# One third of an adaLN vector moved from TensorE's matmuls to VectorE's sums, and the attention bias rows read in two transfers, in a four-layer diffusion step

## The chip, the cores and the metric

The kernel runs on one core of a Trainium2 chip. The time is that of the whole kernel on the device, in microseconds. Each engine of the core (TensorE, VectorE, ScalarE, GpSimd, SyncE) runs its own instructions in order and waits on semaphores for the others. Transfers are issued from queues (SyncE's and GpSimd's here) and are carried by 16 DMA engines that all the queues share.

## The reference

Four layers run over 128 context tokens and 128 latent tokens of width 1024, all in float32. The part that matters here is the adaLN vector of each layer and the attention of the second layer:

```python
cond_act = jax.nn.silu(cond)                 # one vector for the context, one for the latent tokens
for i in range(DEPTH):
    mod = (cond_act @ ada_w[i] + ada_b[i])   # 1024 x 6144 weights a layer
    sh1, sc1, g1, sh2, sc2, g2 = [mod[..., n * D:(n + 1) * D] for n in range(6)]
    h = rms_norm(x, norm1_g[i]) * (1 + sc1) + sh1
    m = mixer(h)                             # pooling, attention, Fourier, pooling
    x = x + g1 * m
    h = rms_norm(x, norm2_g[i]) * (1 + sc2) + sh2
    x = x + g2 * moe(h)                      # 16 experts, top 2
```

In the attention of the second layer (16 heads of 64) the context tokens attend to each other, and a latent token attends to a window of the 2 x 64 latent grid, with a learned relative bias for each head, and to 128 cached context keys:

```python
bias = rpb[:, row_b[:, None, :, None], col_b[None, :, None, :]]
s_loc = jnp.einsum('brqhd,brkwhd->bhrqkw', q, kg) * ATTN_SCALE + bias[None]
s_loc = jnp.where(valid_col[:, None, :], s_loc, -jnp.inf)
s = jnp.concatenate([s_loc.reshape(B, N_HEADS, R, GRID_W, n_loc), s_ctx], axis=-1)
p = jax.nn.softmax(s, axis=-1)
```

## The kernel before, in words

**Weights.** All weights, 527 MB, pass once through a ring of 12 slots of 1 MB (128 partitions of 2048 columns) and seven side buffers. SyncE's queue issues the transfers in a fixed order (`BEFORE_EXPERTS` ahead of a layer's experts, `GROUP_UNITS` in them). Ahead of each transfer it waits in `room` until the slot's last unit has been used: TensorE counts units in the semaphore `s_used`, and `used(u, l, base)` says what count means that unit `u` is done. As the queue is in order, a slot that comes free late holds back all transfers behind it.

**adaLN.** The 6144 columns of a layer's vector are computed in three thirds of 2048 columns; third `t` belongs to layer `t // 3`. A third has eight ring units, one for each 128 of the 1024 input channels. `ada(t, a, b)` on TensorE multiplies units a to b - 1: four matmuls a unit, with `cact` (128 channels x 32 columns, of which the first two are the context's and the latent tokens' SiLU) as weights and 512 columns of the unit as the moving operand, accumulated in four groups of 32 rows of one bank, `B_ADA`. `ada_rows(t)` on VectorE then adds the bias (`adabr`, brought by GpSimd's queue), `ada_turn(t)` on TensorE transposes the rows and `ada_mods(t)` on VectorE writes them to `mods` (and `grow` for the gates). One bank serves all thirds, so third t + 1 waits until third t has been copied (`s_mod`).

**Attention of the second layer** (`attention` of each engine). TensorE makes queries and keys by channel (`by_channel`), values by token (`by_token`), and for each of eight pairs of heads `scores(hp)`, `turn(hp)` (transposes of the probabilities) and `attend(hp)`. VectorE adds the bias and takes the maximum (`bias_max`), ScalarE exponentiates (`exps`), VectorE normalises (`normalise`), ScalarE copies the transposed probabilities (`copy_turned`), VectorE copies the output (`copy_output`). The order on each engine is written out by hand. TensorE's order puts other matmuls between a pair's scores and its transposes: projections, and pieces of the thirds 4 to 8. After the eighth pair, `project` multiplies by the output weights in two halves of the columns (`cc`), each for the two sequences (`s`), with the gate rows (`gates`) ahead of the second sequence and half of third 8 between the column halves. Third 7 is the second third of the second layer; its result is wanted for the gate and shift that come after attention.

**Bias rows.** In the first layer the relative bias is turned around, written to memory as `bias_rows` (3 grid-row distances x 128 x 16 heads) and in the second layer read back into `braw`: partition p, the query, gets for each key row the 64 x 16 numbers that begin p % 64 rows on. Rows of neighbouring partitions overlap. GpSimd's queue does this right behind the cached keys and values (`ck`, `cv`); VectorE expands `braw` into `bias` (line 1130) ahead of the first `bias_max`.

Of the kernel before, what the change touches and what calls it, by code (L numbers as in the profile page):

```python
# [7 lines left out]
F32 = mybir.dt.float32  # L8
# [6 lines left out]
P = 128  # L15
# [38 lines left out]
def matrix_units(name, c):  # L54
# [7 lines left out]
    + matrix_units("qkv", 4) + ada_units(5) + matrix_units("qkv", 1) + ada_units(6)[:4] + matrix_units("qkv", 3) + ada_units(6)[4:]  # L62
    + matrix_units("qkv", 5) + ada_units(7) + matrix_units("wo", 0) + ada_units(8)[:4] + matrix_units("wo", 1) + ada_units(8)[4:],
# [60 lines left out]
B_ADA = B_G  # L124

# [84 lines left out]
def used(u, l, base):  # L210

    return base * NU + (u + 1 - LAYER_UNITS * l)


def build(nc, x_prompt, x_sample, cache_k, cache_v, c, c_ctx, ada_w, ada_b, norm1_g, norm2_g, pool_w,
# [4 lines left out]
    with ctx:  # L220
# [50 lines left out]
        gpair = sb("gpair", [P, GROUP, 2])  # L271

# [30 lines left out]
        with ExitStack() as at:  # L303
# [4 lines left out]
            qT = sb("qT", [P, DB, T], F32, at)  # L308
            kT = sb("kT", [P, DB, T], F32, at)
# [4 lines left out]
            sb("at_experts", [P, 64], F32, at)  # L314
# [47 lines left out]
        knew = ck  # L362

# [12 lines left out]
        s_used = sem("s_used")  # L376
        s_behind = sem("s_behind")
# [116 lines left out]
        def _(sp):  # L494
# [66 lines left out]
            def group(l, base, k):  # L561
                it = sp.snap(base + k)
                e0 = sp.snap((k & (NG - 1)) * GROUP)
                for v, (kind, e, h) in enumerate(GROUP_UNITS):
                    u = EXPERTS_AT[l] + v
                    sp.wait_ge(s_used, used(u - RING, l, it))
# [22 lines left out]
        def _(pool):  # L589
# [18 lines left out]
            nc.gpsimd.memset(rw[:, :, :], 0.0).then_inc(s_zero, 1)  # L608
            nc.gpsimd.memset(rheads[:, :, :], 0.0).then_inc(s_pad, 1)
            pool.wait_ge(s_zero, 4)  # L610
# [8 lines left out]
            pool.dma_start(bias_dram.rearrange("d p h -> p d h"), rback[:, :, :]).then_inc(s_bias, 16)  # L619
# [35 lines left out]
        def _(ac):  # L655
# [93 lines left out]
            def attention(l, base):  # L749
# [9 lines left out]

                def exps(hp):  # L760
# [16 lines left out]
                empty(Q0, blocks(qT, 0, 2))  # L777
                empty(K0, blocks(kT, 0, 2))
# [12 lines left out]
                empty(Q1A, blocks(qT, 4, 2))  # L791
# [656 lines left out]
        def _(pe):  # L1448
# [130 lines left out]
            def project(l, base, name, src, banks, between=None):  # L1579

                for cc in range(2):
                    if cc == 1 and between is not None:
                        between()
# [511 lines left out]
```

## Time and profile before

| | us |
|---|---|
| median of 3 runs | 1321.14 |
| lowest and highest run | 1320.13, 1322.42 |
| the profiled execution | 1319.5 |
| its span, first to last instruction | 1317.7 |
| TensorE busy in the span | 1247.0 (95%) |
| VectorE busy in the span | 390.7 (30%) |
| ScalarE busy in the span | 330.6 (25%) |

The profiled execution is one run of its own. Busy time counts matmuls and element-wise instructions and not waits or the issue of transfers. The memory is read at 405 GB/s over the whole span. Starts are in microseconds from the span's start.

### The profile page before, as it was taken

Reading aid. Unit: us, or ns where it says so; the run is one execution under the profiler, and the core shown is the slowest. Engines: PE = TensorE matmul, PEld = TensorE weight load, DVE = VectorE, ACT = ScalarE, POOL = GpSimd, SP = SyncE. Lnnn points to the kernel's source line nnn. Section 1 sums busy time; section 2 is a strip of 40 time slices with the busy share of each in tenths; the row PEclk is TensorE's granted clock in tenths of the full one; section 3 lists DMA queues with packets and bytes.
Section 4 is the critical chain, followed back from the end, with each engine's and each line's share of the span. In section 5 each row is a group of like instructions: output and inputs, shape, how many; then the busy total and the mean of one; then the engine's idle time right before and its main releaser. Section 6 shows DMA issues by size and latency. Waiting matters only on the chain.

```text
span 1317.7 us, 17235 instructions
## 1 busy us (share of the span) xinstructions
PE 1247.0 (95%) x6557; PEld 561.7 (43%) x6557; DVE 390.7 (30%) x882; ACT 330.6 (25%) x712; POOL 37.6 (3%) x76
## 2 busy tenths in 40 slices
PE   3979999999899999999999899999999989999996
PEld 0433434343656644443434254443434444434342
DVE  1242213222232324321332324222331452213324
ACT  1241212122221223221212233221222452212122
POOL 2100000000200000000100000000000000000000
PEclk9889999999999999999999999999999999999999
DMA  9999999999999988999999999999999999999994
GB/s 371 420 420 421 421 420 422 421 421 421 400 367 408 394 339 356 422 420 421 421 419 422 421 408 398 422 421 422 420 421 421 413 422 420 422 421 420 422 421 193
DMA packets 87278, 535.43 MB, mean 406 GB/s; under 512 B 11192, under 2 KB 13336, under 8 KB 25760
## 3 DMA queue, kind: packets, MB, share of 16 engines
q1 hardware_dynamic: 82336, 527.47, 97.4%
q0 software_dynamic: 3120, 5.17, 1.2%
q10 hardware_dynamic: 1744, 1.73, 0.4%
q8 instruction: 53, 0.87, 0.3%
q14 instruction: 25, 0.20, 0.0%
HBM read 532.20 MB, written 2.12 MB: 405 GB/s over the span
## 4 chain that ended last, share of the span: by engine, by line
PE 83%; DMA 10%; DVE 3%; ACT 2%; issue 1%; SPq 0%; DVEq 0%; ACTq 0%
PE ps L1954 31%; PE ps L2003 15%; PE ps L1940 5%; PE ps L2015 5%; PE ps L1463 5%; PE ps L1630 4%; PE ps L1592 4%; DMA ring<-in_ada_w_dram 4%; DMA ring<-in_moe_w_up_dram 3%; PE ps L1986 2%; PE ps L1639 2%; DMA ring<-in_attn_wqkv_dram 2%; DMA ring<-in_moe_w_down_dram 2%; PE ps L1560 1%; PE ps L1971 1%; ACT hT L707 1%
## 5 line engine op out<-in xcount | busy, mean ns | idle before, releaser
L1956 PE MATMUL ps<-ring,xg 128*64 128x512 f32 x968 | 438.7, 598 | 0.0
L1954 PE MATMUL ps<-ring,xg 128*64 128x512 f32 x912 | 413.2, 598 | 4.0 <-DMA ring<-in_moe_w_up_dram 4.0
L2003 PE MATMUL ps<-ring,gb 128*64 128x512 f32 x992 | 225.6, 595 | 0.3 <-DMA ring<-in_moe_w_down_dram 0.3
L1954 PEld LDWEIGHTS ps<-ring,xg 128*64 128x64 f32 x912 | 117.7, 137 | 230.0 <-issue 219.6
L1387 DVE SCALAR_TENSOR_TENSOR gb<-ps,gslot,g2x 128x512 f32<-128x512 f32 x128 | 90.2, 746 | 248.8 <-PE ps L2003 248.8
L2003 PEld LDWEIGHTS ps<-ring,gb 128*64 128x64 f32 x992 | 68.9, 137 | 134.2 <-issue 126.2
L1956 PEld LDWEIGHTS ps<-ring,xg 128*64 128x64 f32 x968 | 125.0, 137 | 0.0
L885 ACT ACTIVATE y_hi<-gb 128x512 fp32r<-128x512 f32 x128 | 77.2, 627 | 169.0 <-PE ps L2015 109.1
L1463 PE MATMUL ps<-ring,cact 128*32 128x512 f32 x768 | 94.8, 629 | 12.1 <-ACT cact L668 6.0
L872 ACT ACTIVATE gu<-ps 128x512 f32<-128x512 f32 x64 | 38.3, 598 | 247.0 <-PE ps L1956 247.0
L1396 DVE TENSOR_TENSOR y_lo<-gb,y_hi 128x512 fp32r<-128x512 f32 x128 | 83.6, 688 | 12.5 <-ACT y_hi L885 11.9
L1378 DVE TENSOR_TENSOR gb<-sg,ps 128x256 f32<-128x256 f32 x64 | 26.8, 418 | 192.7 <-ACT sg L877 192.7
L877 ACT ACTIVATE sg<-ps 128x256 f32<-128x256 f32 x64 | 24.6, 384 | 216.6 <-PE ps L1986 216.6
L2015 PE MATMUL ps<-y_hi,onehotT 64*128 64x512 f32 x256 | 57.5, 446 | 3.1 <-DVE y_lo L1396 3.1
L1404 DVE TENSOR_TENSOR gpair<-onehotT 128x8 f32<-128x8 f32 x16 | 2.7, 168 | 194.0 <-ACT onehotT L891 194.0
L1630 PE MATMUL ps<-hT,ring 128*128 128x256 f32 x256 | 58.2, 389 | 2.0 <-DMA ring<-in_attn_wqkv_dram 2.0
L1940 PE MATMUL ps<-onehot,h_hi 128*128 128x256 f32 x256 | 56.7, 304 | 3.1 <-DVE adabr L1024 3.1
L868 ACT ACTIVATE xg<-ps 128x512 f32<-128x512 f32 x64 | 38.2, 597 | 77.4 <-PE ps L1940 77.3
L1630 PEld LDWEIGHTS ps<-hT,ring 128*128 128x128 f32 x256 | 49.4, 194 | 9.7 <-issue 2.7
L1463 PEld LDWEIGHTS ps<-ring,cact 128*32 128x32 f32 x768 | 22.5, 114 | 71.4 <-issue 52.1
L1940 PE MATMUL ps<-onehot,h_lo 128*128 128x256 f32 x256 | 52.4, 287 | 0.0
L2015 PE MATMUL ps<-y_lo,onehotT 64*128 64x512 f32 x256 | 50.4, 391 | 0.0
(223 smaller groups left out, 1117.9 us busy)
## 6 DMA issues: line engine op xcount, KB each, us to landing
ring<-in_moe_w_down_dram SPq DMA_DIRECT2D x124, 1024.0 KB, 17.7
ring<-in_moe_w_up_dram SPq DMA_DIRECT2D x121, 1024.0 KB, 16.9
ring<-in_moe_w_gate_dram SPq DMA_DIRECT2D x114, 1024.0 KB, 17.9
ring<-in_ada_w_dram SPq DMA_DIRECT2D x96, 1024.0 KB, 17.9
ring<-in_attn_wqkv_dram SPq DMA_DIRECT2D x12, 1024.0 KB, 21.5
spare<-in_moe_w_down_dram SPq DMA_DIRECT2D x4, 1024.0 KB, 23.6
xh<-in_moe_w_up_dram SPq DMA_DIRECT2D x4, 1024.0 KB, 20.9
hT<-in_moe_w_gate_dram SPq DMA_DIRECT2D x4, 1024.0 KB, 22.7
```

What stands on the lines that cost most here:

```text
L872: nc.scalar.activation(gu[:, :, :], ps[:, B_GU, :].rearrange("p (m j) -> p j m", j=FB), ACT.Copy).then_inc(s_guc, 1)
L885: nc.scalar.activation(y_hi[:, s, :], y[:, s, :], ACT.Copy).then_inc(s_yh, 1)
L1387: v.scalar_tensor_tensor(y[:, s, :], ps[:, DOWN_BANKS[e % 2], :], gslot[:, e:e + 1], g2x[:, s, :], ALU.mult, ALU.mult).then_inc(s_yf, 1)
L1396: v.tensor_tensor(y_lo[:, s, :], y[:, s, :], y_hi[:, s, :].bitcast(F32), ALU.subtract).then_inc(s_y, 1)
L1463: mm = pe.matmul(ps[32 * j:32 * (j + 1), B_ADA, :], cact[:, i, :], w[:, j * 512:(j + 1) * 512], start=(i == 0 or (t, i) == (3, 4)), stop=( ...
L1592: mm = pe.matmul(ps[:, banks[2 * cc + s], :], src[4 * h + b][:, s * SEQ:(s + 1) * SEQ], w[:, b * 512:(b + 1) * 512], start=(h == 0 and b = ...
L1630: mm = pe.matmul(ps[:, JOB_BANK[i], d * T:(d + 1) * T], w[b // 4][:, at:at + P], hT[:, b, :], start=(b == 0), stop=(b == DB - 1))
L1940: mm = pe.matmul(ps[:, (B_G, B_T)[j % 2], d * 256:(d + 1) * 256], h[:, s, b * P:(b + 1) * P], onehot[:, s, :, 0:SLOTS], start=(n2 == 0), s ...
L1954: mg = pe.matmul(ps[0:SLOTS, B_GU, :], xg[:, b, e, :], wg[:, i * F:(i + 1) * F], start=(b == 0), stop=(b == DB - 1))
L1956: mu = pe.matmul(ps[SLOTS:P, B_GU, :], xg[:, b, e, :], wu[:, i * F:(i + 1) * F], start=(b == 0), stop=(b == DB - 1))
L2003: mm = pe.matmul(ps[r * SLOTS:(r + 1) * SLOTS, DOWN_BANKS[e % 2], :], acts[:, e % ACTS, j, :], w[:, i * D + r * HALF:i * D + (r + 1) * HAL ...
L2015: mm = pe.matmul(ps[:, B_ACC + 2 * s + r, :], onehotT[part, NSEQ * e + s, 0:SEQ], of[part, s, :], start=False, stop=False, skip_group_chec ...
```

## The change

Third 7 no longer runs as 32 matmuls of TensorE. VectorE multiplies each unit (128 channels x 2048 columns) by its channel's SiLU, a scalar per partition, and adds up the eight units, once for each of the two sequences, into two tiles of 128 x 2048: 2 products and 14 multiply-adds (`summed`). They are put one by one between the instructions of the softmax, from the fourth pair on. One tile is `spare`, the other the place of the first eight query and key blocks, which are no longer wanted then; queries and keys are laid out anew for that. TensorE then sums each tile over its 128 partitions with a column of ones (`reduce_sums`, 8 matmuls) inside the output projection. Slots of third 7 are freed by VectorE's count `s_summed`. The units of third 7 move forward in the ring's order, the last four units of third 6 move behind the eighth pair's scores, and the transposes of thirds 6 and 7 move with them.

The bias rows are written to memory in three transfers instead of one, in reverse order of the distance, and read in two transfers over 128 partitions (one for each key row) instead of four over 64.

```diff
 BEFORE_EXPERTS (second layer)
-    + matrix_units("qkv", 4) + ada_units(5) + matrix_units("qkv", 1) + ada_units(6)[:4] + matrix_units("qkv", 3) + ada_units(6)[4:]
-    + matrix_units("qkv", 5) + ada_units(7) + matrix_units("wo", 0) + ada_units(8)[:4] + matrix_units("wo", 1) + ada_units(8)[4:],
+    + matrix_units("qkv", 4) + ada_units(5) + matrix_units("qkv", 1) + ada_units(7)[:1] + ada_units(6)[:4] + ada_units(7)[1:3]
+    + matrix_units("qkv", 3) + ada_units(7)[3:4] + matrix_units("qkv", 5) + ada_units(7)[4:6] + ada_units(6)[4:] + ada_units(7)[6:]
+    + matrix_units("wo", 0) + ada_units(8)[:4] + matrix_units("wo", 1) + ada_units(8)[4:],
...
+        sums = [spare[:, :], first_qk[:, :, :, :].rearrange("p i b t -> p (i b t)")]
...
 SyncE, room
-                    sp.wait_ge(s_used, used(USE_OF[at - RING], l, base))
+                    u = USE_OF[at - RING]
+                    if u in SUMMED_UNITS:
+                        sp.wait_ge(s_summed, NSEQ * SUMMED_UNITS[u])
+                    else:
+                        sp.wait_ge(s_used, used(u, l, base))
...
 GpSimd
-            pool.dma_start(bias_dram.rearrange("d p h -> p d h"), rback[:, :, :]).then_inc(s_bias, 16)
+            for d in range(3):
+                pool.dma_start(bias_dram[2 - d], rback[:, d, :]).then_inc(s_bias, 16)
...
-            pool.wait_ge(s_bias, 32)
-            for r in range(2):
-                for kr in range(2):
-                    src = bass.AP(tensor=bias_dram.tensor, offset=((kr - r + 1) * P + 1) * HEADS,
-                                  ap=[[HEADS, GRID_W], [1, GRID_W * HEADS]])
-                    pool.dma_start(braw[r * GRID_W:(r + 1) * GRID_W, kr, :, :].rearrange("p k h -> p (k h)"), src).then_inc(s_bias, 16)
+            pool.wait_ge(s_bias, 64)
+            for kr in range(2):
+                src = bass.AP(tensor=bias_dram.tensor, offset=((1 - kr) * P + 1) * HEADS,
+                              ap=[[P * HEADS, 2], [HEADS, GRID_W], [1, GRID_W * HEADS]])
+                pool.dma_start(braw[:, kr, :, :].rearrange("p k h -> p (k h)"), src).then_inc(s_bias, 16)
...
 VectorE
+            def summed(i, seqs=range(NSEQ)):
+                at = place(UNIT_AT[("ada", SUMMED, i)], 1)
+                w = ring[:, at % RING, :]
+                if 0 in seqs:
+                    v.wait_ge(s_slot[at % RING], landed(at, 1, bases[1]))
+                for s in seqs:
+                    if i == 0:
+                        ins = v.tensor_scalar(sums[s], w, cact[:, i, s:s + 1], None, ALU.mult)
+                    else:
+                        v.wait_ge(s_summed, NSEQ * (i - 1) + s + 1)
+                        ins = v.scalar_tensor_tensor(sums[s], w, cact[:, i, s:s + 1], sums[s], ALU.mult, ALU.add)
+                    ins.then_inc(s_summed, 1)
...
                 normalise(3)
-                empty(Q1B, blocks(qT, 6, 2))
+                v.wait_ge(s_job, JOB_DONE[K_TURN0])
+                summed(0)
+                empty(Q1B, second(0, 2))
+                summed(1)
                 copy_output(2)
+                summed(2)
+                summed(3, [0])
                 copy_output(3)
                 bias_max(4)
+                summed(3, [1])
                 normalise(4)
-                empty(K1B, blocks(kT, 6, 2))
+                empty(K1B, second(1, 2))
+                summed(4, [0])
                 bias_max(5)
+                summed(4, [1])
                 normalise(5)
-                ada_rows(6, l, base)
+                summed(5, [0])
                 bias_max(6)
+                summed(5, [1])
                 normalise(6)
-                ada_mods(6)
+                summed(6, [0])
                 empty(V1B, vtok[:, 1, 512:1024])
+                summed(6, [1])
                 copy_output(4)
                 bias_max(7)
                 copy_output(5)
                 normalise(7)
+                ada_rows(6, l, base)
                 copy_output(6)
                 copy_output(7)
+                ada_mods(6)
+                summed(7)
                 ada_rows(7, l, base)
                 ada_mods(7)
                 projected(l, "wo", 0, (4, 5, 6, 7))
...
 TensorE
+            def reduce_sums():
+                pe.wait_ge(s_mod, SUMMED)
+                pe.wait_ge(s_summing, 2)
+                pe.wait_ge(s_summed, NSEQ * ADA_UNITS)
+                for s in range(NSEQ):
+                    for j in range(4):
+                        mm = pe.matmul(ps[32 * j:32 * (j + 1), B_ADA, :], summing[:, 31 - s:63 - s], sums[s][:, j * 512:(j + 1) * 512],
+                                       start=(s == 0), stop=(s == NSEQ - 1))
+                mm.then_inc(s_reduced, 1)
...
                 scores(5)
-                ada(6, 4, ADA_UNITS, l, base)
                 w = weights(5)
                 by_token(V1A, w, 0)
...
-                turned(K_TURN1, [kT[:, 4 + i, 0:SEQ] for i in range(4)])
-                ada_turn(6)
+                turned(K_TURN1, [kT[4 + i][:, 0:SEQ] for i in range(4)])
                 by_token(V1B, w, 1)
...
                 attend(5)
-                ada(7, 0, 6, l, base)
+                ada(6, 4, ADA_UNITS, l, base)
                 turn(7)
                 attend(6)
-                ada(7, 6, ADA_UNITS, l, base)
                 attend(7)
                 gates(l, 0)
-                ada_turn(7)
+                ada_turn(6)
                 pe.wait_ge(s_os, PAIRS)
-                project(l, base, "wo", oT, (4, 5, 6, 7), lambda: ada(8, 0, 4, l, base))
+                project(l, base, "wo", oT, (4, 5, 6, 7),
+                        {(0, 1, 0): reduce_sums, (0, 1, 1): lambda: ada_turn(7), (1, 0, 0): lambda: ada(8, 0, 4, l, base)})
```

## Rows read from the trace of the kernel before

**Rows 1.** Stretches: us, busy time of each engine, granted clock, DMA share, GB/s.

```profile
480.00:495.00 15.00, 15.00 (x45) 6.03 (x47) 1.57 (x3) 5.61 (x10) 1.63 (x4) 1.00 0.81 329
530.00:733.00 203.00, 203.00 (x1043) 83.16 (x1043) 50.73 (x105) 43.90 (x84) 3.62 (x7) 1.00 1.01 421
```

**Rows 2.** SyncE's queue: start us, us, the transfer issued.

```profile
495.04 0.33 SPq L496 DMA_DIRECT2D ring<-in_moe_w_gate_dram  x1
```

**Rows 3.** TensorE in order of time: start us, us, what [idle before it].

```profile
444.36 3.64 PE L1463 MATMUL ps<-ring,cact 128*32 128x512 f32 x32
468.60 5.36 PE L1463 MATMUL ps<-ring,cact 128*32 128x512 f32 x48
475.49 1.92 PE L1463 MATMUL ps<-ring,cact 128*32 128x512 f32 x16
479.84 3.60 PE L1592 MATMUL ps<-ring,o_first 128*128 128x512 f32 x8
```

**Rows 4.** VectorE in order of time, columns as in rows 3.

```profile
373.00 3.76 DVE L1130 SCALAR_TENSOR_TENSOR gb<-braw,kattn 128x1024 f32<-128x1024 f32 x2 [3.68 <-DMA braw<-bias_rows]
378.04 0.42 DVE L1103 TENSOR_REDUCE r_ge<-ps 128x2 f32<-128x256 f32 x1 [1.27 <-PE ps L1657]
381.73 1.03 DVE L1114 TENSOR_TENSOR soft<-soft,r_ge 128x256 f32<-128x256 f32 x2
421.88 0.69 DVE L1093 COPY qT<-ps 128x512 f32<-128x512 f32 x1 [3.18 <-PE ps L1630]
```

**Rows 5.** VectorE's groups by form: shapes, count, busy us, mean ns.

```profile
L1444 DVE SCALAR_TENSOR_TENSOR x<-x,rs,gain 128x512 f32<-128x512 f32 x2 | 1.4, 741 | 0.0
L1045 DVE TENSOR_TENSOR x<-x,gb 128x512 f32<-128x512 f32 x12 | 8.3, 692 | 0.4
L1104 DVE TENSOR_TENSOR ps<-ps,gb 128x256 f32<-128x256 f32 x8 | 3.4, 422 | 0.0
L981 DVE TENSOR_SCALAR xh<-x,rs 128x512 f32<-128x512 f32 x16 | 7.1, 484 | 0.3
```

**Rows 6.** The chain that ended last, 335 to 420 us.

```profile
377.92 1.19 issue
379.12 7.11 PE ps L1639 x16
386.66 0.66 PE ps L1666 x6
```

**Rows 7.** GpSimd's transfers in order of issue: start us, us, what.

```profile
348.80 0.56 POOL L625 DMA_DIRECT2D ck<-in_cache_k_dram  x1 [288.13 <-ACT qT L755]
349.35 0.54 POOL L626 DMA_DIRECT2D cv<-in_cache_v_dram  x1
349.88 2.11 POOL L632 DMA_DIRECT2D braw<-bias_rows  x4
```

**Rows 8.** The bias rows' four transfers.

```profile
DMA to landing us min/median/max: 13.9/17.6/21.5
```

**Rows 9.** Issues of 335 to 500 us: count, KB each, median us to landing.

```profile
ck<-in_cache_k_dram POOLq DMA_DIRECT2D x1, 512.0 KB, 8.0
cv<-in_cache_v_dram POOLq DMA_DIRECT2D x1, 512.0 KB, 11.3
```

**Rows 10.** DMA packets by queue: 355 to 362 us, then 361 to 373 us.

```profile
DMA packets 503, 2.74 MB, mean 392 GB/s; under 512 B 59, under 2 KB 59, under 8 KB 277
q1 hardware_dynamic: 253, 1.85, 69.7%
q0 software_dynamic: 250, 0.89, 34.3%
...
DMA packets 983, 3.23 MB, mean 269 GB/s; under 512 B 263, under 2 KB 263, under 8 KB 772
```

**Rows 11.** Two stretches behind a wait of TensorE, columns as in rows 1.

```profile
338.00:342.00 4.00, 2.96 (x7) 2.34 (x8) 1.30 (x5) 2.54 (x7) 0.00 (x0) 0.65 1.07 398
342.00:346.00 4.00, 4.00 (x19) 3.49 (x18) 0.00 (x0) 0.00 (x0) 0.00 (x0) 0.92 1.02 414
```

More of the change, by code:

```diff
@@ L124 @@
 B_ADA = B_G
+SUMMED = 7
+SUMMED_UNITS = {UNIT_AT[("ada", SUMMED, i)]: i + 1 for i in range(ADA_UNITS)}
 TURNED_BANKS = [B_T, B_Y, B_G]
@@ L210, in used @@
 def used(u, l, base):
-    return base * NU + (u + 1 - LAYER_UNITS * l)
+    return base * NU + (u + 1 - LAYER_UNITS * l - sum(1 for of in SUMMED_UNITS if of <= u))
 def build(nc, x_prompt, x_sample, cache_k, cache_v, c, c_ctx, ada_w, ada_b, norm1_g, norm2_g, pool_w,
@@ L362, in build @@
         knew = ck
+        qT, kT = [[(first_qk, second_qk)[b // 4][:, i, b % 4, :] for b in range(DB)] for i in range(2)]
+        sums = [spare[:, :], first_qk[:, :, :, :].rearrange("p i b t -> p (i b t)")]
         ps = ctx.enter_context(nc.psum_tensor("ps", [P, 8, 512], F32))
@@ L565, in group @@
                     u = EXPERTS_AT[l] + v
[L566 removed]
+                    sp.wait_ge(s_used, used(EXPERTS_AT[l], l, it) + (v - RING))
                     sp.sem_inc(s_issue, 1)
@@ L758, in blocks, with second, first @@
                     return of[:, b:b + n, :].rearrange("p d t -> p (d t)")
+                def second(i, b):
+                    return blocks(second_qk[:, i, :, :], b, 2)
+                def first(i, b):
+                    return blocks(first_qk[:, i, :, :], b, 2)
                 def exps(hp):
@@ L790, in attention @@
                 exps(2)
-                empty(Q1A, blocks(qT, 4, 2))
+                empty(Q1A, second(0, 0))
                 copy_turned(2)
@@ L795, in attention @@
                 copy_turned(3)
-                empty(K1A, blocks(kT, 4, 2))
+                empty(K1A, second(1, 0))
                 exps(4)
@@ L1096, in blocks, with second, first @@
                     return of[:, b:b + n, :].rearrange("p d t -> p (d t)")
+                def second(i, b):
+                    return blocks(second_qk[:, i, :, :], b, 2)
+                def first(i, b):
+                    return blocks(first_qk[:, i, :, :], b, 2)
                 def bias_max(hp):
@@ L1577, in pool_tokens, with project @@
                               start=True, stop=True).then_inc(s_pm, 1)
[L1579 removed]
+            def project(l, base, name, src, banks, between):
                 for cc in range(2):
[L1582 to L1583 removed]
                     for s in range(NSEQ):
[L1585 to L1588 removed]
                         for h in range(2):
+                            if (cc, s, h) in between:
+                                between[cc, s, h]()
+                            if (cc, s, h) == (0, 1, 0):
+                                gates(l, 1)
+                            if cc == 1 and h == 0:
+                                pe.wait_ge(s_g2x, 2 * l + 2)
                             w = unit(UNIT_AT[(name, cc, h)], l, base)
@@ L1690, in attention @@
                 emptied(K0 + 1)
-                turned(K_TURN0, [kT[:, i, 0:SEQ] for i in range(4)])
+                turned(K_TURN0, [kT[i][:, 0:SEQ] for i in range(4)])
                 ada(4, 0, ADA_UNITS, l, base)
@@ L1796, in fourier @@
                 pe.wait_ge(s_f2d, 4)
-                project(l, base, "four", [fT[:, b, :] for b in range(DB)], (4, 5, 6, 7), lambda: ada(10, 0, 4, l, base))
+                project(l, base, "four", [fT[:, b, :] for b in range(DB)], (4, 5, 6, 7),
+                        {(1, 0, 0): lambda: ada(10, 0, 4, l, base)})
                 ada(10, 4, ADA_UNITS, l, base)
```

33 lines of the change are left out of this document (19 added, 14 removed).

## The prediction

> **What bounds the kernel now.** I read the stretches first. In the attention stage of the second layer (about 339 to 516 us) TensorE is busy without a gap while the DMA engines run short of work: 329 GB/s in 480 to 495 us against 421 GB/s in 530 to 733 us [rows 1]. The ring of weights is full there, so transfers wait for TensorE to free slots. The transfer queue shows it: the next layer's first expert weights are issued at 495.04 us [rows 2], when TensorE ends the first half of the output projection, begun at 479.84 us [rows 3]. From there the stream runs at its full rate for over 200 us, so a microsecond won or lost by TensorE ahead of 495 us moves that stream, and with it the rest of the kernel, by the same amount.
>
> Next comes TensorE's own order [rows 3]: the pieces of the adaLN third that moves are the 48 matmuls at 468.60 us (5.36 us) and the 16 at 475.49 us (1.92 us). The reader is to see that each stands where TensorE would otherwise wait for a softmax.
>
> Then VectorE. Its waits between the steps of the softmax stand in brackets [rows 4], and its instructions by form give the price of the new sums [rows 5].
>
> Last, the start of attention, for the bias rows. In the chain, TensorE waits 1.19 us at 377.92 us for the third pair of attention weights, and turns the first softmax at 386.66 us [rows 6]. VectorE waits 3.68 us for the bias rows until 373.00 us, expands them in 3.76 us, waits 1.27 us more for the first scores at 378.04 us and ends the first normalisation at 381.73 + 1.03 = 382.76 us [rows 4].
>
> **The change, part by part.**
>
> *Off TensorE.* The third's 64 matmuls go: 5.36 + 1.92 = 7.28 us, less some 0.15 us in which pipelined ends overlap, 7.1 us. In comes the reduction: 8 matmuls, 16 in the trace's passes, of the same 32 columns by 512; the row of 16 gives 1.9 us. The transposes and gates are only moved. Net 5.2 us.
>
> *Onto VectorE.* Two products and 14 multiply-adds, each over 2048 columns. A multiply-add from SBUF with a scalar per partition takes 741 ns at 512 columns; two-input forms rise from 422 ns at 256 columns to 692 at 512, 1.055 ns a column, so 741 + 1536 x 1.055 = 2.36 us. Below stands the pure slope, 2.16 us; above, the slowest row, 1.88 us for 1024 strided columns [rows 4], would give 3.8 us. These operands are contiguous like the 741 ns row, so I take 2.35. The two products go by the 484 ns row: that less a fixed part of 0.15 (692 - 512 x 1.055 ns), four times, plus 0.15 is 1.5 us, and 2.35 the upper bound; 1.5 taken, as it is the same operation [rows 5]. Sum some 36 us, beside TensorE.
>
> *What they delay.* I laid them into VectorE's order with TensorE's times moved up by what leaves. Up to the fifth softmax all is hidden: the products end before the copy at 421.88 us [rows 4], the next five sums before the fourth output. The fifth bias and maximum start 1.5 us later than their scores, and the normalisation is still ready when the value projection, 7.1 us long, ends. Then it is tight: the copy that empties the last value projection is 0.6 us late, the fourth and fifth outputs 0.3, the last softmax 0.3 (the four units of the third before, 3.6 us of the four at 444.36 us, now cover it), and the last attention product waits 0.5 for an output copy that the removed 16 matmuls used to cover. Together 1.7 us, 0.8 at 2.16 us a sum. The last two sums end some 2 us before the reduction wants them, behind 7 us of projection; what waits behind the reduction on VectorE (the first residual piece) has no reader near. Gain: 5.2 - 1.7 = 3.5 us, bounds 2.5 and 4.5.
>
> *Weights' order.* The units of the moved third come earlier in the ring and are freed by VectorE; each is freed before the queue would otherwise ask for its slot (a queue waits meanwhile for the fifth and sixth attention pairs). Nothing.
>
> *Bias rows, written.* Three transfers for one at 38 us, some 1.5 us more on GpSimd's queue; the rows behind are wanted much later. Nothing.
>
> *Bias rows, read.* This decides. Before, four transfers of 256 KB, each 64 rows on both sides, follow the two cached-key and value transfers on GpSimd's queue [rows 7]; they land about 363 to 373 us (13.9 us after its issue for the first, 21.5 for the last [rows 8]). Now two of 512 KB. On the SBUF side each has 128 rows, but its source pattern counts 2, then 64, then 1024. How such a pattern is cut over the 16 DMA engines no row of before shows: the large transfers here count 64 or 128 first on both sides. I bound it by all sixteen engines and by two, a half each, since 2 and 128 share no larger cut. I lean to two: every large transfer that lands fast here has one outer count of 64 or 128 on both sides, and a finer cut of the new ones would have to cross the source's outer count of 2 while the destination has a single count.
>
> With sixteen: the cached values are of the same size and land 3.85 us after the keys (349.35 + 11.3 against 348.80 + 8.0 us [rows 7, 9]), so both end by 360.65 + 7.7 = 368.4 us, earlier than now.
>
> With two: 256 KB go through one engine. In 355 to 362 us queue 0 (GpSimd's) and queue 1 (the weights) exchange packets one for one, 250 against 253, and queue 0 moves 0.89 MB in 7 us [rows 10], 8 KB per us and engine. 256 KB take 31 (by the pace of the cached values) to 33 us: 391 to 393 us. The attention weights then queued come in 2 KB rows, so packets between are shorter: I take 390 us. Bounds: 10 us with the engine to itself (421 GB/s over 16), landing at 371; the pace of the four old transfers, some 9 us for three, 16 KB each an engine, gives 49 us, landing at 409.
>
> The Trainium skill ("DMA: Bandwidth & Descriptors", section "Why a DMA increments its semaphore by 16 and not by 1") says that the engines are the largest number up to 16 that divides the slowest counts of both sides, which is 2 here, with an exception for some plain copies from GpSimd. By it the sum is that with two engines, about 1331 us, against 1316 with sixteen; no run here shows it.
>
> *What a late landing costs.* From landing to the normalised softmax: 382.76 - 373.00 - 1.27 = 8.5 us; TensorE wants it at 386.5, so the rows may land until 378.0 us free. At 390 it waits 12.0 us, with everything in order behind it (the third before it needs VectorE's sum behind the same maximum, so TensorE has nothing to run). After a wait TensorE starts at half clock: behind the wait that ends at 339 us the granted clock is 0.65 for four microseconds and 0.92 for the next four [rows 11], that is 2.8 + 0.6 = 3.4 us at 1.2 of 2.4 GHz, which costs 1.7 us. Weights on the two or four laden engines come a few us later than now, but they are next wanted after 395 us, inside the wait. Cost 13.7 us.
>
> *Sum.* 1319.5 (the profiled execution: span 1317.7) - 3.5 + 13.7 = 1329.7 us. That execution lies 1.6 us under the median of the runs shown, 1321.14, so about 1331.
>
> **The rivals.**
>
> *All sixteen engines carry the bias rows (faster).* For it: the destination does have 128 rows, and the old transfers, 64 rows each, coincide with the one stretch where engines are busy and yet move only 269 GB/s (361 to 373 us), where the 128-row keys and values just before leave 392 [rows 10]. Whole-width transfers would remove that, the third pair of weights would come 1.2 us sooner [rows 6], and the sum is -3.5 - 1.2: 1314.8, or 1316.4 beside the median. It decides if they land by 378 us; from 381.5 us on the gain is gone, sooner with the clock. The Trainium skill ("DMA: Bandwidth & Descriptors", section "Rules for kernel authors") advises one transfer over 128 partitions in place of two over halves; the trace, with 269 against 392 GB/s, agrees.
>
> *Two engines, but quick.* Landing between 371 and 381 us: 1317 to 1321.
>
> *Both transfers on the same two engines.* 512 KB each, landing near 420 us: 1360.
>
> *VectorE becomes the bound.* Each sum 3.8 us: from the copy at 421.88 us on every softmax is late, by 7 us at the fifth and some 18 in all; 1319.5 + 13, or more with late rows. Sums up to 2.9 us would still pay. The 741 ns row speaks against.
>
> *The work saved is not given on.* The time stays if transfers, not TensorE, held the stream; 495.04 us [rows 2] speaks against.
>
> **How the numbers follow.** Two engines at the shared pace 0.63; sixteen 0.23; two but quick 0.05 (0.02 of it faster); the same two 0.05; VectorE 0.02; not given on 0.02. A measurement here can tell 0.2%, 2.6 us. Faster 0.25, same 0.05, slower 0.70. The likeliest's own range is 1326 to 1337 (landing 385 to 396 us); with the sixteen-engine case the whole range is 1315.5 to 1337, which leaves out the slowest landings.
>
> **What would show it.** A landing of the bias rows near 390 us, VectorE idle before their expansion, TensorE idle some 12 us ahead of the first softmax's transposes and then a stretch at half clock. Later, sums of 2.35 us each, no third's matmuls between the last softmaxes, a reduction of 1.9 us inside the output projection, and the first expert transfer 3.5 us earlier, counted from those transposes. The forecast is wrong if the rows land before 378 us.

## The result, and the profile after

| | before | after |
|---|---|---|
| median, run side by side (4 runs each) | 1320.92 us | 1340.41 us |
| profiled execution, its span | 1319.5, 1317.7 us | 1340.89, 1339.1 us |
| after over before, 95% interval | | 1.0144, 1.013 to 1.0157 |

The change makes the kernel 19.5 us slower by the medians, 21.4 by the two profiled executions. The direction was forecast, the time (1331, at most 1337) was not.

The page of the changed kernel: its span, what the DMA engines moved in each of 40 slices of the span, and the count of packets. Below it stand the same rows of the kernel before.

```profile
span 1339.1 us, 17157 instructions
...
GB/s 371 420 420 421 422 420 421 421 421 416 397 321 211 394 345 336 414 421 420 421 420 422 420 409 404 422 421 420 421 422 420 415 420 421 421 421 420 420 422 200
DMA packets 89102, 535.44 MB, mean 400 GB/s; under 512 B 12984, under 2 KB 15160, under 8 KB 27584
```

```profile
GB/s 371 420 420 421 421 420 422 421 421 421 400 367 408 394 339 356 422 420 421 421 419 422 421 408 398 422 421 422 420 421 421 413 422 420 422 421 420 422 421 193
DMA packets 87278, 535.43 MB, mean 406 GB/s; under 512 B 11192, under 2 KB 13336, under 8 KB 25760
```

Only the twelfth and thirteenth slices (368 to 435 us) fall far behind: 321 and 211 GB/s against 367 and 408. The stream of weights runs short there. So I read the bias rows next: GpSimd's queue and the tile's landings, then VectorE in order of time.

```profile
350.00 1.64 POOL L648 DMA_DIRECT2D braw<-bias_rows  x2
```

```profile
DMA to landing us min/median/max: 22.8/37.4/52.0
```

```profile
402.78 3.68 DVE L1175 SCALAR_TENSOR_TENSOR gb<-braw,kattn 128x1024 f32<-128x1024 f32 x2 [33.34 <-DMA braw<-bias_rows]
406.49 0.42 DVE L1148 TENSOR_REDUCE r_ge<-ps 128x2 f32<-128x256 f32 x1
410.18 1.03 DVE L1159 TENSOR_TENSOR soft<-soft,r_ge 128x256 f32<-128x256 f32 x2
```

Issued within a microsecond of before [rows 7], the rows land at 402.8 us instead of 373.0 [rows 4]. VectorE stands still for 33.34 us ahead of their expansion, where it waited 3.68, and the maximum behind it waits for nothing: the scores have long been there. The landings (22.8 and 52.0 us after issue) are counted by one semaphore that both transfers share, so only the last is sure.

TensorE in order of time:

```profile
388.97 9.68 PE L1708 MATMUL ps<-ring,hT 128*128 128x512 f32 x16 [10.93 <-issue]
408.93 1.12 PE L1549 MATMUL ps<-const,rows 128*128 128x128 f32 x4 [10.29 <-DVE rows L1048]
411.36 1.51 PE L1735 MATMUL ps<-const,soft 128*128 128x128 f32 x6 [1.31 <-DVE soft L1159]
421.55 3.64 PE L1521 MATMUL ps<-ring,cact 128*32 128x512 f32 x32
...
495.05 0.87 PE L1735 MATMUL ps<-const,soft 128*128 128x128 f32 x6 [0.28 <-DVE soft L1159]
497.35 0.66 PE L1745 MATMUL ps<-pT,vtok 128*64 128x128 f32 x8 [0.62 <-DVE hT L1164]
...
506.68 1.07 PE L1532 MATMUL ps<-spare,summing 128*32 128x512 f32 x8
507.56 1.04 PE L1532 MATMUL ps<-first_qk,summing 128*32 128x512 f32 x8
```

The third pair of value weights comes at 389 us instead of 379.12 [rows 6]; that wait is spent inside the longer one. The first softmax's transposes begin at 411.36 us, 24.7 us later than at 386.66 [rows 6]. Three stretches (columns as in rows 1), of which the clock is the reading:

```profile
376.00:387.00 11.00, 2.03 (x24) 0.88 (x16) 0.00 (x0) 0.00 (x0) 0.00 (x0) 0.70 1.02 288
387.00:412.00 25.00, 11.43 (x23) 5.28 (x24) 7.62 (x11) 2.21 (x9) 2.06 (x4) 0.64 0.79 289
412.00:425.00 13.00, 13.00 (x65) 5.82 (x63) 3.61 (x9) 2.53 (x9) 0.00 (x0) 0.90 0.21 70
```

Granted were 0.70 and 0.64 of the full clock while TensorE mostly waited (0.64 means that the lower of its two levels, 1.2 of 2.4 GHz, had some 18 of the 25 us), and 0.90 in the 13 us of work behind: it comes back to the higher level only some way into them. The same 32 adaLN matmuls that began at 395.18 us in the kernel before,

```profile
395.18 3.64 PE L1463 MATMUL ps<-ring,cact 128*32 128x512 f32 x32
```

begin at 421.55 us now: 26.4 us late, so the slow clock costs 1.7. From there the change earns: the first expert transfer goes out 22.2 us later than in [rows 2], so 4.2 us were won back between.

```profile
517.21 0.33 SPq L505 DMA_DIRECT2D ring<-in_moe_w_gate_dram  x1
```

VectorE's new sums, by form, are what they were costed at, and the products a little less (1.28 us each):

```profile
L1038 DVE SCALAR_TENSOR_TENSOR spare<-ring,cact,spare 128x2048 f32<-128x2048 f32 x7 | 16.4, 2345 | 0.0
L1038 DVE SCALAR_TENSOR_TENSOR first_qk<-ring,cact,first_qk 128x2048 f32<-128x2048 f32 x7 | 16.4, 2345 | 0.0
```

Last, DMA packets by queue (packets, MB, share of 16 engines' time) in 361 to 369, 371 to 383 and 387 to 401 us:

```profile
q1 hardware_dynamic: 739, 2.59, 92.7%
q0 software_dynamic: 740, 0.15, 11.7%
...
q1 hardware_dynamic: 579, 2.86, 86.8%
q0 software_dynamic: 723, 0.49, 17.4%
...
q1 hardware_dynamic: 901, 4.91, 96.6%
q0 software_dynamic: 291, 0.23, 5.6%
```

GpSimd's queue (q0) moves 19 KB per us in the first stretch, 41 in the second, 16 in the third: two laden engines at 9.4 KB per us and engine, near the 8 of [rows 10], then about four, then two at 8.2. In the first it makes as many packets as the weights' queue (q1), 740 against 739, but they carry next to nothing.

### The profile page after: what moved, and what is told of

It reads as the page before. It is cut to its first block, busy times and chain, and to the rows that moved or that the text cites. A ratio compares the mean times of both kernels' runs of the same rounds, so it can differ in the third digit from the quotient of the medians.

```text
span 1339.1 us, 17157 instructions
## 1 busy us (share of the span) xinstructions
PE 1248.1 (93%) x6509; PEld 563.3 (42%) x6509; DVE 424.7 (32%) x898; ACT 330.5 (25%) x712; POOL 38.2 (3%) x78
## 2 busy tenths in 40 slices
DMA packets 89102, 535.44 MB, mean 400 GB/s; under 512 B 12984, under 2 KB 15160, under 8 KB 27584
## 4 chain that ended last, share of the span: by engine, by line
PE 83%; DMA 7%; DVE 4%; another core or an unknown queue 2%; ACT 2%; issue 1%; SPq 0%; DVEq 0%; ACTq 0%
PE ps L2022 32%; PE ps L2071 15%; PE ps L2008 5%; PE ps L2083 5%; PE ps L1699 4%; PE ps L1661 4%; DMA ring<-in_ada_w_dram 4%; PE ps L1521 3%; PE ps L2054 3%; DMA ring<-in_attn_wqkv_dram 2%; PE ps L1708 2%; DMA ring<-in_moe_w_down_dram 1%; PE ps L1629 1%; PE ps L2039 1%; ACT hT L723 1%
## 5 line engine op out<-in xcount | busy, mean ns | idle before, releaser
L1521 PE MATMUL ps<-ring,cact 128*32 128x512 f32 x704 | 86.6, 624 | 13.7 <-DMA ring<-in_ada_w_dram 8.5
## 6 DMA issues: line engine op xcount, KB each, us to landing
ring<-in_attn_wqkv_dram SPq DMA_DIRECT2D x12, 1024.0 KB, 22.2
```

The source lines that it names most:

```text
L1521: mm = pe.matmul(ps[32 * j:32 * (j + 1), B_ADA, :], cact[:, i, :], w[:, j * 512:(j + 1) * 512], start=(i == 0 or (t, i) == (3, 4)), stop=( ...
```

## The experiments

The theory: the first count of the new source pattern, 2, leaves each transfer to two DMA engines, and the late rows are the whole loss. The rivals: VectorE's sums cost the time; the size or number of the transfers; the memory that they read. "Lands" is the start of the expansion, as VectorE waits for the rows there unless it is said otherwise. Ratios are over the kernel before on the same chip. The diffs are shortened to the lines and patterns that matter.

**Only the reading undone.**

```diff
+            for r in range(2):
                 for kr in range(2):
-                    ap=[[P * HEADS, 2], [HEADS, GRID_W], [1, GRID_W * HEADS]]   # to braw[:, kr]
+                    ap=[[HEADS, GRID_W], [1, GRID_W * HEADS]]                   # to braw[r * 64:(r + 1) * 64, kr]
```

> The changed kernel, but the bias rows are read back in four transfers of 64 rows as before the change; everything else of the change stays. Theory (the two new read transfers, whose source pattern counts 2 first, are carried by few DMA engines, and the late rows are the whole loss): the rows land near 373 us, the first softmax is turned near 386.7 us, and what is left is the gain of the moved third, 4.2 us by the two traces: 1316 to 1317.5 us, 0.3% under the kernel before. Rival (VectorE's sums and the new order of weights cost the time, and the late rows only fill a wait that would be there anyway): still about 1335 to 1340 us.

Measured: 1316.92 us, 0.997 (0.9959 to 0.9982). VectorE, TensorE and SyncE's queue:

```profile
371.56 3.77 DVE L1176 SCALAR_TENSOR_TENSOR gb<-braw,kattn 128x1024 f32<-128x1024 f32 x2 [3.24 <-DMA braw<-bias_rows]
...
378.74 7.11 PE L1709 MATMUL ps<-ring,hT 128*128 128x512 f32 x16 [1.82 <-issue]
386.12 0.82 PE L1736 MATMUL ps<-const,soft 128*128 128x128 f32 x6
...
491.36 0.33 SPq L505 DMA_DIRECT2D ring<-in_moe_w_gate_dram  x1
```

The rows are back at 371.56 us, the first transposes at 386.12, and with all the sums still there the kernel is faster than before the change. The rival of the sums is out.

**Only the reading (and writing) of the rows, in the kernel before.** The diff is the GpSimd part of the change and nothing else.

> The kernel before, with nothing of the change but the writing and reading of the bias rows. Theory: the rows land near 403 us instead of 373, the first softmax is turned 24 to 26 us later, and with the half clock behind the wait the time is 1343 to 1347 us, above the changed kernel by the 4 us that the moved third gains. Rival (the sums cost the time): 1321 to 1326 us. Rival (both are needed, since the third moved forward in the ring competes with the rows for the DMA engines): between, 1330 to 1335 us, with the rows landing near the 390 us of the prediction.

Measured: 1344.08 us, 1.0182 (1.0166 to 1.0197); landing 400.7 us. The loss needs nothing of the moved third.

**Two transfers of 512 KB with 64 first.**

```diff
-            for kr in range(2): ap=[[P * HEADS, 2], [HEADS, GRID_W], [1, GRID_W * HEADS]]    # to braw[:, kr]
+            for r in range(2):  ap=[[HEADS, GRID_W], [-P * HEADS, 2], [1, GRID_W * HEADS]]   # to braw[r * 64:(r + 1) * 64]
```

> The changed kernel with two read transfers of 512 KB, as in the change, but each for 64 partitions and both key rows, so that the source pattern counts 64 first and 2 second. Theory (the first count decides how many DMA engines carry a transfer): sixteen engines, landing near 373 us, 1316 to 1318 us, like the four transfers. Rival (two transfers of 512 KB with a pattern of three counts are slow because of their size or their number): landing near 400 us and 1338 to 1342 us, like the changed kernel.

Measured: 1316.8 us, 0.997 (0.9958 to 0.9981), landing 370.5 us. Neither size, number nor a third count matters; what stands first does. Its page:

```profile
DMA packets 87311, 535.43 MB, mean 407 GB/s; under 512 B 11193, under 2 KB 13369, under 8 KB 25793
```

That is 11193 packets under 512 B, against 12984 with the same number of transfers in the changed kernel: 1791 of them come with the 2 in front, as many as 64 on each of 14 engines for two transfers (1792).

**Each transfer cut into four along the columns.**

```diff
+                for n in range(4):
-                    ap=[[P * HEADS, 2], [HEADS, GRID_W], [1, GRID_W * HEADS]]
+                    ap=[[P * HEADS, 2], [HEADS, GRID_W], [1, GRID_W * HEADS // 4]]
```

> The changed kernel, each of the two read transfers cut along its columns into four of 128 KB; the source pattern still counts 2, 64 and then 256 columns instead of 1024. It asks whether every such transfer goes to the same few DMA engines or whether successive ones take others. If they take others in turn, eight transfers of two engines each spread over all sixteen: landing at 370 to 380 us and 1316 to 1320 us. If it is always the same engines: landing at 403 us or later, 1340 us or more. If only two alternating pairs are used, as the landing of the two transfers near 403 us allows too: near 403 us and 1340 us.

Measured: 1336.54 us, 1.0115 (1.01 to 1.0131), landing 397.9 us.

```profile
DMA packets 89198, 535.46 MB, mean 401 GB/s; under 512 B 13080, under 2 KB 15256, under 8 KB 27680
```

By these expectations the eight transfers stay on few engines; the next ones give another reading, below.

**One of the two transfers.** The first key row as in the change, the second in two transfers of 64 rows.

> The changed kernel, but only the first key row is read in the changed form (one transfer of 512 KB whose source counts 2, 64, 1024); the second comes in two transfers of 64 rows, as before the change, behind it. It asks whether the two transfers of the change go to the same two DMA engines, or to two each. Theory A (two each, four in all): one such transfer takes as long as two, so the rows land near 400 us and the time stays at 1336 to 1340 us. Theory B (both go to the same two engines, which give the weights little room): half the bytes on them, landing near 361 + 21 = 382 us, a wait of 4 us and half a stretch at half clock: 1319 to 1324 us.

Measured: 1329.54 us, 1.0062 (1.0043 to 1.0082), landing 388.65 us, between the theories' times.

```profile
DMA packets 88222, 535.44 MB, mean 403 GB/s; under 512 B 12104, under 2 KB 14280, under 8 KB 26704
```

The packets under 512 B are 12104, that is 912 over the kernel before: 16 for one transfer more, as in the other counts, and 896 = 14 x 64. Here the third pair of weights came at 390.7 us, after the rows, and TensorE waited 14.6 us for it: a lag of the laden engines' weights that the change itself hides.

**The 64 rows written as 2 x 32, and as 8 x 8,** in four transfers of 64 rows.

> The changed kernel with the bias rows in four transfers of 64 rows, as before the change, but the 64 rows of the source written as 2 times 32, so that the same bytes go from the same places to the same places and only the pattern's first count differs. Theory (the first count decides): two DMA engines for each transfer, 14 that move next to nothing, so some 4 x 14 x 32 = 1,792 more packets under 512 B than the 11,224 of the four plain transfers, a landing at 385 to 405 us and 1325 to 1342 us. Rival (the pattern is joined into one count of 64 again, or the count has no part in it): landing near 371 us, 1316 to 1318 us, 11,224 such packets.

> As the experiment with 2 times 32, with the 64 rows of the source written as 8 times 8. Theory (the first count decides): eight DMA engines for each transfer and eight that move next to nothing, 4 x 8 x 8 = 256 more packets under 512 B than 11,224, and a landing little later than with sixteen, at 371 to 380 us: 1316 to 1321 us. Rival (only a count of 2 hurts, or the counts are joined): 371 us and 11,224 packets. Rival (any pattern of three counts falls to two engines): 385 us or later.

One run each: 1318.54 and 1316.31 us, landing 371.0 and 370.7 us, 11224 packets under 512 B in both, as with plain rows. The counts seem to be joined again where the steps allow it, so these two tell nothing of the theory.

**Counts of 4, 8 and 16 that can't be joined.** With n pieces a key row:

```diff
-            for d in range(3):
-                pool.dma_start(bias_dram[2 - d], rback[:, d, :])
+            for kr in range(2):
+                for j in range(n):      # m = 128 // n queries
+                    r, first = j // (n // 2), 1 + m * (j % (n // 2))
+                    pool.dma_start(bias_dram[n * kr + j, 0:m + 63], rback[first:first + m + 63, 1 + kr - r, :])
...
+            ap=[[P * HEADS, n], [HEADS, m], [1, GRID_W * HEADS]]
```

> The changed kernel, still two read transfers of 512 KB over 128 partitions. The rows that they read are written in the first layer in 4 pieces a key row, a piece of memory for 32 queries each, at one distance, so that the source of a transfer counts 4, 32, 1024 and the counts can't be joined. Theory (as many DMA engines carry a transfer as its first counts allow, the others make a small packet for each row in its place): 4 engines a transfer, 128 KB on each, 2 x 12 x 32 = 768 more small packets than the plain ones, and the second transfer starts once other engines are through the 32 small packets of the first, some 4 us late; at 8 to 9 KB per us and engine the rows land at 376 to 382 us and the time is 1316 to 1320 us. Rival (any first count other than 64 or 128 goes to two engines): 403 us, 1340 us.

> As the experiment with a count of 4, with 8 pieces a key row, for 16 queries each: the source counts 8, 16, 1024. Theory: 8 engines a transfer, 64 KB on each, 2 x 8 x 16 = 256 more small packets, landing at 368 to 373 us and 1314.5 to 1317 us. Rival (two engines): 403 us, 1340 us.

> As the experiment with a count of 4, with 16 pieces a key row, for 8 queries each: the source counts 16, 8, 1024. Theory: all 16 engines, no small packets in the place of data, the whole width of 128 partitions as with the rows laid out one by one, but without the 2 MB of traffic of that: landing near 368 us, some 400 GB/s in 361 to 373 us, no wait ahead of the third pair of value weights, 1314 to 1315.5 us, the fastest of all. Rival (only rows laid out one by one do this): 371 us or later, 1316.5 us or more.

| first count | landing | after first issue | time | ratio (interval) |
|---|---|---|---|---|
| 2 (the change) | 402.8 us | 52.8 us | 1340.41 | 1.0144 (1.013 to 1.0157) |
| 4 | 381.7 | 31.7 | 1322.26 | 1.0011 (1.0002 to 1.002) |
| 8 | 376.7 | 27.4 | 1318.92 | 0.9986 (0.9976 to 0.9995) |
| 16 | 371.1 | 22.2 | 1317.05 | 0.9966 (0.9953 to 0.9979) |
| 64 (two transfers) | 370.5 | 22.3 | 1316.8 | 0.997 (0.9958 to 0.9981) |

The landing follows the count as the theory says, but less closely than I expected: with 8 and 16 the rows land some 3 us later than forecast (376.7 and 371.1 us), and 4 and 8 cost 2 us more. That 16 over 128 partitions is not better than 64 was a miss.

The small packets bear the theory out closely. The pages count 12168, 11912 and 12168 under 512 B with 4, 8 and 16. These versions write their pieces in 8, 16 and 32 small transfers, and GpSimd's queue makes 32 packets for each (512, 768 and 1280 packets in 30 to 110 us). Without these, the queue's other fixed packets and 16 for each read, 768, 256 and none are left: 2 x 12 x 32, 2 x 8 x 16 and 0, a packet for each row on each engine that carries no data.

**Rows laid out one by one in the first layer**, then plain transfers of 128 rows, 128 counted first on both sides:

```diff
+            for kr in range(2):
+                for r in range(2):   # ap=[[HEADS, GRID_W], [1, GRID_W * HEADS]], memory to memory
+                    pool.dma_start(bias_full[kr, r * GRID_W:(r + 1) * GRID_W], src)
...
+                pool.dma_start(braw[:, kr, :, :].rearrange("p k h -> p (k h)"), bias_full[kr])
```

> The changed kernel, but the bias rows are laid out in memory in the first layer already (four transfers of 256 KB from memory to memory, some 65 us after the start, so that each of 128 queries has its 64 x 16 numbers in a row of its own), and read in two transfers that count 128 rows on both sides. This is the case of sixteen engines and the whole width that the prediction held as a rival. By it: landing near 368 us, above 350 GB/s in 361 to 373 us instead of some 296, no wait of 1 to 2 us ahead of the third pair of value weights, and a time 1 to 2 us under that of four transfers of 64 rows, 1315 to 1316 us, less what 2 MB more of traffic in the first layer cost (up to 5 us, if the stream of weights is the bound there: 1317 to 1321 us). Rival (64 or 128 rows make no difference): the same landing near 371 us and the same wait.

Measured: 1314.64 us, 0.9959 (0.9946 to 0.9973), the lowest of all, though the next intervals overlap it. In 361 to 373 us it moves 404 GB/s (columns as in rows 1), and the wait ahead of the third pair of weights is gone:

```profile
361.00:373.00 12.00, 12.00 (x74) 9.03 (x77) 3.76 (x3) 3.50 (x5) 0.00 (x0) 1.00 1.02 404
...
378.46 7.13 PE L1712 MATMUL ps<-ring,hT 128*128 128x512 f32 x16
```

**Is it the width or the memory?** Rows one by one, read over 64 partitions; with a gap, so that 2, 64, 1024 are counted; and with gaps for 16, 8, 1024.

```diff
+ four64:  for r, kr: braw[r * 64:(r + 1) * 64, kr] <- bias_full[kr, r * 64:(r + 1) * 64]
+ gap:     ap=[[65 * GRID_W * HEADS, 2], [GRID_W * HEADS, 64], [1, GRID_W * HEADS]]
+ 16x8:    ap=[[9 * GRID_W * HEADS, 16], [GRID_W * HEADS, 8], [1, GRID_W * HEADS]]
```

> The bias rows laid out one by one in memory in the first layer, as in the experiment that did so, but read in four transfers of 64 rows instead of two of 128. It asks why that experiment alone moved more than 400 GB/s in 361 to 373 us: because its transfers cover 128 partitions (the prediction's reason), or because its rows are 1 MB of separate memory instead of windows that overlap within a few KB. By the width: some 270 to 305 GB/s in that stretch, landing near 371 to 373 us, a wait of 1 to 3 us ahead of the third pair of value weights, 1316 to 1318 us. By the separate memory: above 350 GB/s, landing at 370 us or before, no such wait, 1314 to 1315.5 us.

> Rows laid out one by one, with a gap of one row between the two halves, so that a read transfer over 128 partitions counts 2, 64, 1024 as in the change, but reads separate memory. It asks whether the overlapping windows have a part in the slow landing of the change. Theory (the first count of 2 alone): two engines a transfer, 1,792 more small packets, landing at 395 to 405 us, 1335 to 1341 us. Rival (two engines are slow because they read overlapping memory): landing at 380 to 388 us, 1318 to 1326 us.

> Rows laid out one by one with a gap after each eighth, so that a read transfer over 128 partitions counts 16, 8, 1024 and reads separate memory. Of the two transfers over 128 partitions carried by sixteen engines, the one with rows one by one moved 404 GB/s beside the weights in 361 to 373 us, the one with a count of 16 over overlapping windows 305. If overlapping memory is the difference: some 400 GB/s here, no wait for the rows, 1314 to 1316 us. If the pattern is (three counts instead of two): some 270 to 310 GB/s, a wait of 3 us for the rows, 1317 to 1320 us.

Measured: 1319.18 (0.999, 0.9981 to 0.9999), 1343.15 (1.0169, 1.0154 to 1.0185) and 1318.77 us (0.9984, 0.9974 to 0.9994). With the gap the rows land 52.4 us after the first issue, like the change's 52.8: the overlapping windows have no part in it. The DMA packets of 361 to 373 us, over 64 partitions and with the count of 16:

```profile
DMA packets 730, 3.42 MB, mean 285 GB/s; under 512 B 132, under 2 KB 132, under 8 KB 464
```

```profile
DMA packets 784, 3.58 MB, mean 298 GB/s; under 512 B 173, under 2 KB 173, under 8 KB 489
```

Neither separate memory nor 128 partitions alone gives 404 GB/s. It takes 128 rows in one count; why, no run shows. With the same time from issue to landing (23.2 and 22.0 us) as the four transfers of 64 rows (22.7) and the count of 16 over windows (22.2), the two versions without a leading 2 are some 2 us slower than those. What they add is the 2 MB of traffic in the first layer, and in the four traces with such rows the first read is issued at 350.5 to 352.0 us, against 347.8 to 350.0 in the others; no run separates this further. In both traces TensorE waits for the third pair of value weights (1.93 and 2.29 us), and the projection behind takes 8.80 us at a granted clock of 0.88 (376 to 390 us); with plain rows over 128 partitions it takes 7.13 at 1.00.

**VectorE's sums cut to 64 of 2048 columns,** in the version with four read transfers of 64 rows; the rest of the sums is left out.

```diff
-                ins = v.scalar_tensor_tensor(sums[s], w, cact[:, i, s:s + 1], sums[s], ...)
+                ins = v.scalar_tensor_tensor(sums[s][:, 0:64], w[:, 0:64], cact[:, i, s:s + 1], sums[s][:, 0:64], ...)
```

> The changed kernel with four read transfers of 64 rows, and VectorE's 14 multiply-adds cut to 64 of their 2048 columns, so that most of the third's sum is left out. It prices what VectorE's sums cost TensorE. The prediction put this at 1.7 us (0.8 at the lower price of a sum); the waits of the trace with whole sums give 0.29 + 0.62 = 0.9 us that were not there before. Theory: 0.9 to 1.7 us under the version with whole sums, 1315 to 1316 us. Rival (the sums are hidden in full): 1316.5 to 1317 us. Rival (sums of 2.35 us cost far more, all that the removal could have given): 1313 us or less.

Measured: 1316.47 us, 0.9968 (0.9958 to 0.9978), the same as with whole sums (1316.92). The waits of 0.29 and 0.62 us that the version with whole sums has ahead of its last softmax's transposes and its last attention product stay (0.44 and 0.62), so they are not the sums' doing but the lost cover of the matmuls that left.

## Why the prediction was right and wrong

**Right: the mechanism and the sign.** Two engines a transfer was the likeliest case at 0.63, and the small packets (14 x 64 a transfer), the pace and the counts of 2, 4, 8 and 16 bear it out. What the Trainium skill ("DMA: Bandwidth & Descriptors", section "Why a DMA increments its semaphore by 16 and not by 1") says on the largest number that divides the slowest counts agrees with the landings of that table; its exception for some plain GpSimd copies does not apply to this pattern.

**Wrong: the term of the landing.** The step that failed is "256 KB take 31 (by the pace of the cached values) to 33 us: 391 to 393 us", cut to 390: it lets both transfers start at once. The rows landed at 402.8, so TensorE's wait was not 12.0 but 402.8 - 378.0 = 24.8 us; measured at the transposes, 24.7. With it the sum comes out: 1319.5 - 4.2 + 24.8 + 1.7 = 1341.8, against 1340.89 measured.

The pace was near (9.4 KB per us and engine in the first stretch, 8.2 in the last, against 8). What I left out are the turns that an engine spends on the other transfer. On an engine that carries no data of a transfer that transfer still makes packets, 64 by the count above, and each takes its turn against one weight packet (740 against 739 in 361 to 369 us). So the engines of the second transfer first worked off 64 empty turns: 128 turns in place of 64. The trace shows the late start. GpSimd's queue moves two engines' worth of data until 367 us; then, in 367 to 369 and 369 to 371 us:

```profile
q0 software_dynamic: 265, 0.05, 17.8%
...
q0 software_dynamic: 370, 0.09, 27.6%
```

That is 25 and 45 KB per us: at about 369 us the second pair of engines gets to its data. Estimates from these times: the 64 empty turns took some 8 us from the cached values' landing (349.46 + 11.3 = 360.8 us), and the 64 with data the 34 us from 369 to 402.8. The late start is most of the 12.8 us by which the landing was missed; the rest is the cut to 390, for which no row spoke, and a pace a little slower. With one such transfer, and two plain ones behind it, the rows land at 388.65 us, close to the 390 that I had worked out for 64 turns.

The eight pieces agree more loosely. Their 13080 packets under 512 B are 96 more than the change has (16 for each of six transfers more), so 1792 small ones again, now 16 on an idle engine for each piece: whichever engines carry the data, each has 8 x 16 = 128 turns, and the rows land 48.1 us after the first issue. Put by turns an engine, 16, 32, 64 and 128 end 22.2, 27.4, 31.7 and 48 to 52.8 us after the first issue, some 0.25 us a turn on the mean (estimate: (48.1 to 52.8 - 22.2) / 112). A turn has no single price: an empty one took some 0.13 us in the change (8 us for 64), the mean of the eight pieces' turns, most of them empty, nearly 0.3 (360.5 to 397.9 us for 128), and no run shows why. That the empty turns are the cause of the late start is argued from the counts and from that step; no run takes the small packets away and leaves the two engines. The Trainium skill ("DMA: Bandwidth & Descriptors", section "Why a DMA increments its semaphore by 16 and not by 1") says that GpSimd's transfers with fewer than 16 engines go to the next ones in turn; the four engines' worth of 371 to 383 us agrees, and it also means that I should not have let both transfers start at once without asking what the second pair did meanwhile.

**Right: what a late landing costs.** Free until 378.0 us, then microsecond for microsecond, and the 1.7 us forecast for the slow clock: 24.8 + 1.7 = 26.5 against 26.4 measured at the adaLN matmuls behind the first softmax.

**Right, with a small miss: the gain.** 3.5 us was forecast (2.5 to 4.5), 4.2 measured from those adaLN matmuls to SyncE's transfer, and 3.9 by the medians with the old reading. The sums took 2.345 us (2.35 forecast), the products 1.28 (1.5), the reduction 1.07 + 1.04, overlapped to 1.9 (1.9). Of the lateness of 1.7 us, the 0.3 at the last softmax and 0.5 at the last attention product came as 0.28 and 0.62; the 0.6 at the last value projection and 0.3 at two outputs did not come. The gain is then 5.2 - 0.9 = 4.3 us.

**Weights on laden engines** were called a few us later; they were ten. The wait for the rows covered that, but with one new transfer they became the wait that ended last.

**The rival of sixteen engines** (1316.4 us) was a fair price: 1314.64 where 128 plain rows are read at once, 1316.8 to 1319.18 in the other versions with at least 16 counted first. Its reason, the width of 128 partitions, holds only half: 404 GB/s with 128 rows in one count, but 298 and 305 with 16 counted first. The Trainium skill ("DMA: Bandwidth & Descriptors", section "Rules for kernel authors") advises one transfer over 128 partitions in place of two halves; the runs agree with that only for the plain one.

**The range** failed because its upper end was set at 1337 and not by the upper bound that I had worked out for the landing (409 us, which would have given about 1350): I had taken that bound as unlikely, without a row that said so.

## What to carry to other kernels

Read a transfer's pattern from the outside in: put a count that 16 divides first, on both sides; a leading count of 2 turned a read of 22 us into one of 53. Count an engine's turns, empty packets among them, and not its bytes alone, where it shares with a full stream. And when two independent edits ship together, run each alone: here one was worth -4 us (1316.92 against 1320.84) and the other +23 (1344.08).

## What the runs showed that I had not expected

- A transfer on two engines isn't free on the other fourteen: it makes 896 small packets there (12104 against 11192 + 16 under 512 B), and beside a full stream as many packets as the weights made (740 against 739 in 8 us).
- Cutting such transfers into four along their columns gains little: landing 48.1 us after the first issue, against 52.8.
- With plain 128-row transfers the DMA engines move 404 GB/s in all in 361 to 373 us, with the other forms that count 16 or 64 first 269 (the kernel before) to 305, whether 64 or 128 partitions wide.
